# A one-core decoder-layer kernel: the first element's key transposes and scores move into the last steps of the prompt attention, and GpSimd's queue is reordered

## What is computed

```python
# prompt: causal, over its own 512 keys
s = einsum('bqhmd,bkhmd->bhmqk', qi, k) * scale
w = softmax(s)[:, :, 0] - lam * softmax(s)[:, :, 1]
o = einsum('bhqk,bkhv->bqhv', w, v)
# sample: 8 elements, each with 1024 past keys in 8 pages and 8 new ones
k_past = cache_k[l, page_table]; v_past = cache_v[l, page_table]
w = _diff_weights(concatenate([s_past, s_new]), lam)
o = w[..., :P] @ v_past + w[..., P:] @ v_new
# both: a root mean square norm over each head's 128 values
o = o * rsqrt(mean(o * o) + LN_EPS) * g * (1 - lam_init)
```

## Time and profile before

| | us |
|---|---|
| Median of 3 runs | 699.65 |
| The profiled execution, its own time | 696.74 |
| Its span, first to last instruction | 695.1 |
| Matmuls on TensorE, busy | 604.1 (87%) |
| VectorE, busy | 267.1 (38%) |
| ScalarE, busy | 158.5 (23%) |
| GpSimd, busy | 104.5 (15%) |
| TensorE's share of the chain that ended last | 67% |

### The profile page before, as it was taken

The page is one execution under the profiler, slowest core; times in us unless marked ns, Lnnn a source line. Parts: engine busy times, 40 slices in busy tenths (PEclk is TensorE's granted clock), DMA queues, the critical chain, the costliest instruction groups (busy, mean ns, idle before and its releaser), DMA issues.

```text
span 695.1 us, 10925 instructions
## 1 busy us (share of the span) xinstructions
PE 604.1 (87%) x3948; PEld 390.5 (56%) x3948; DVE 267.1 (38%) x566; ACT 158.5 (23%) x321; POOL 104.5 (15%) x189
## 2 busy tenths in 40 slices
PE   6999999997997789899999889898998777777674
PEld 5777677455666577665554546566565443444331
DVE  1562259318555555544735661111011000000267
ACT  2001452125235344341000111111111111111122
POOL 6000000012104343500100012121121111110100
PEclk9999999999999999999999899999999999999997
DMA  9630301328107889950498959999999999999683
GB/s 252 212 104 20 121 1 36 116 91 318 62 1 246 321 295 384 394 196 1 171 425 346 397 223 370 420 415 417 414 416 417 417 419 414 417 417 411 236 300 124
DMA packets 57135, 186.93 MB, mean 269 GB/s; under 512 B 10643, under 2 KB 14739, under 8 KB 48386
## 3 DMA queue, kind: packets, MB, share of 16 engines
q1 hardware_dynamic: 43440, 151.44, 56.4%
q0 software_dynamic: 11328, 29.01, 11.3%
q10 hardware_dynamic: 2322, 5.90, 2.1%
HBM read 176.80 MB, written 18.42 MB: 281 GB/s over the span
## 4 chain that ended last, share of the span: by engine, by line
PE 67%; SPq 12%; DMA 6%; DVE 6%; issue 5%; ACT 3%; ACTq 0%; POOLq 0%; DVEq 0%
PE ps L755 12%; PE ps L1081 10%; PE ps L1005 6%; PE ps L1104 6%; SPq L410 4%; PE ps L804 4%; PE ps L769 4%; PE ps L876 4%; DMA arena<-in_w_down_e_dram 4%; SPq L406 3%; PE ps L888 2%; SPq L407 2%; PE ps L912 2%; PE ps L958 2%; PE ps L1031 2%
## 5 line engine op out<-in xcount | busy, mean ns | idle before, releaser
L1081 PE MATMUL ps<-arena 128*64 128x256 f32 x1088 | 122.5, 380 | 17.8 <-DMA arena<-in_w_up_e_dram 17.0
L1081 PEld LDWEIGHTS ps<-arena 128*64 128x64 f32 x1088 | 87.8, 137 | 57.3 <-DMA arena<-in_w_up_e_dram 18.5
L1802 DVE TENSOR_TENSOR arena<-ps,arena 128x128 f32<-128x128 f32 x34 | 9.9, 291 | 203.9 <-ACT arena L1347 203.9
L755 PE MATMUL ps<-arena 128*128 128x288 f32 x352 | 85.9, 407 | 0.1
L1104 PE MATMUL ps<-arena 128*64 128x512 f32 x272 | 62.1, 597 | 23.2 <-DMA arena<-in_w_down_e_dram 10.9
L755 PEld LDWEIGHTS ps<-arena 128*128 128x128 f32 x352 | 66.7, 190 | 18.8 <-issue 0.5
L1104 PEld LDWEIGHTS ps<-arena 128*64 128x64 f32 x272 | 21.5, 136 | 52.9 <-issue 52.9
L547 POOL DMA_DIRECT2D arena<-in_cache_v_dram x64 | 34.6, 541 | 60.4 <-issue 37.8
L655 POOL DMA_INDIRECT y_rows<-arena x17 | 17.2, 1012 | 171.4 <-ACT arena L1354 154.9
L1005 PE MATMUL ps<-arena 128*128 128x512 f32 x96 | 42.7, 596 | 0.0
L876 PE MATMUL ps<-arena 128*128 128x128 f32 x256 | 36.2, 280 | 2.9 <-ACT arena L1284 2.1
(11 more groups left out here) (322 smaller groups left out, 772.8 us busy)
## 6 DMA issues: line engine op xcount, KB each, us to landing
arena<-in_w_gate_e_dram SPq DMA_DIRECT2D x34, 1024.0 KB, 16.3
arena<-in_w_up_e_dram SPq DMA_DIRECT2D x34, 1024.0 KB, 23.6
arena<-in_w_down_e_dram SPq DMA_DIRECT2D x34, 1024.0 KB, 24.7
arena<-in_cache_k_dram SPq DMA_DIRECT2D x64, 256.0 KB, 7.7
arena<-in_cache_v_dram POOLq DMA_DIRECT2D x64, 256.0 KB, 6.6
arena<-in_w_in_dram SPq DMA_DIRECT2D x4, 2048.0 KB, 8.4
arena<-in_w_out_dram SPq DMA_DIRECT2D x2, 2048.0 KB, 15.9
x_rows<-arena ACTq DMA_DIRECT2D x8, 512.0 KB, 8.8
```

Source lines behind the costliest of these rows:

```text
L755: last = mm(ps[:, b + h, 0:HALF], win[n % 2][:, k, m * P:(m + 1) * P], xT[:, k, h * HALF:(h + 1) * HALF], start=k == 0, stop=k == KD - 1)
L1081: last = mm(ps[fh * 64:fh * 64 + 64, u, 0:256], xTm[:, k, u * CAP:(u + 1) * CAP], gu[:, :, k, fh * P:(fh + 1) * P], start=k == 0, stop=k = ...
```

## The change

- Element 0's 8 pages of keys are transposed inside the rounds 7, 8 and 9 of the prompt attention (`first_keys`, three, three and two pages), into PSUM bank 5, and pages 4 and 6 into bank 3. ScalarE copies all eight (`first_keys_out`) into a new buffer `kT0`, which lies where the projections' input was.
- The 64 new keys in `kT0` and the zeros behind them are written by GpSimd. Those of `kT` are written by VectorE as before, now in `sample(0)` behind the maximum.
- Element 0's scores are issued ahead of the values of step 10. The transposes of the end states move from round 7 to round 10.
- In GpSimd's stream the first query copy comes forward, and `query(1)` and the last root (`row_scale(NT - 2)`) come ahead of `values(1)`, of the four stores and of `values(2)`. Before, `values(1)` stood in the middle of the prompt attention.

```diff
+        kT0 = area(A_XT, NH, 1152)
@@ GpSimd
             row_scale(0)
             row_scale(1)
-            values(1, lambda: q.wait_ge(s_pj, 33))
+            q.wait_ge(s_pj, 33)
+            g.tensor_copy(kT0[:, :, PAST:PAST + TS], kTn[:, :, SEQ:T]).then_inc(s_k0n, 1)
+            g.memset(kT0[:, :, PAST + TS:], 0.0).then_inc(s_k0n, 1)
             row_scale(2)
+            q.wait_ge(s_cst, 3)
+            g.tensor_copy(qcur, qd[:, 0, :, :]).then_inc(s_qc, 1)
...
+            query(1)
+            row_scale(NT - 2)
+            values(1, lambda: q.wait_ge(s_sc, 1))
             q.wait_ge(s_endc, 1)
             q.dma_start(O["h_prompt"][0], ends_out[0:1, :]).then_inc(s_out, 16)
...
             values(2, tails_free)
-            query(1)
-            row_scale(NT - 2)
             query(2)
@@ TensorE
+            def first_keys(g):
+                if g == 0:
+                    pe.wait_ge(s_kin[0], 16 * NPG)
+                    pe.wait_ge(s_pev[1], 32)
+                elif g <= 3:
+                    pe.wait_ge(s_ktc[(g - 1) % 2], (g - 1) // 2 + 1)
+                else:
+                    pe.wait_ge(s_ktc[g % 2], g // 2)
+                if g == 4:
+                    pe.wait_ge(s_exp, len(STEPS) - 1)
+                for h in range(NH):
+                    last = tr(ps[:, 3 if g >= 4 and g % 2 == 0 else 5, h * P:(h + 1) * P], kpages[0][g][:, h * P:(h + 1) * P], ident)
+                last.then_inc(s_ktp[g % 2], 1)
...
             for n in range(len(STEPS)):
...
-                if n == 7:
+                if n == 10:
                     ends_rows()
+                if n in (7, 8):
+                    first_keys(3 * (n - 7))
+                if n == 9:
+                    first_keys(6)
                 if n + 1 < len(STEPS):
                     transposes(n + 1)
+                if n in (7, 8):
+                    first_keys(3 * (n - 7) + 1)
+                if n == 9:
+                    first_keys(7)
                 values(n)
+                if n == 9:
+                    first_scores()
+                if n in (7, 8):
+                    first_keys(3 * (n - 7) + 2)
...
-            for g in range(NPG):
-                keys_transpose(0, 0, g, True)
-            pe.wait_ge(s_dc, 2)
-            sample_scores(0)
             sample(0, 0, first=True)
@@ ScalarE
+            def first_keys_out(g):
+                act.wait_ge(s_ktp[g % 2], g // 2 + 1)
+                a.copy(kT0[:, :, g * P:(g + 1) * P], ps[:, 3 if g >= 4 and g % 2 == 0 else 5, :].rearrange("p (h c) -> p h c", h=NH)).then_inc(s_ktc[g % 2], 1)
...
-            for g in range(0, NPG, 2):
-                keys_out(0, g)
@@ VectorE
-            dve.wait_ge(s_pvp, len(STEPS))
-            link(v.tensor_copy(kT[:, :, PAST:PAST + TS], kTn[:, :, SEQ:T]))
-            link(v.memset(kT[:, :, PAST + TS:], 0.0))
-            dve.sem_inc(s_dc, 1)
+            def new_keys():
...
                 v.tensor_reduce(coef[:, u:u + 1], ps[:, 0:3, 0:384], AX.XY, ALU.max, negate=True).then_inc(s_mxs, 1)
+                if first:
+                    new_keys()
...
-            for g in range(1, NPG, 2):
-                keys_out(0, g)
```

More of the change, by code:

```diff
@@ L602, in tails_free @@
                 q.wait_ge(s_dc, 2)
+                q.wait_ge(s_k0n, 2)
                 q.wait_ge(s_out, 16 * 6)
-            values(2, tails_free)
             query(1)
             row_scale(NT - 2)
+            values(1, lambda: q.wait_ge(s_sc, 1))
+            q.wait_ge(s_endc, 1)
+            q.dma_start(O["h_prompt"][0], ends_out[0:1, :]).then_inc(s_out, 16)
+            q.dma_start(O["h_sample"][0], ends_out[1:9, :]).then_inc(s_out, 16)
+            q.dma_start(O["conv_prompt"][0, 0], ends_out[9:12, :]).then_inc(s_out, 16)
+            q.dma_start(O["conv_sample"][0].rearrange("b j c -> (b j) c"), ends_out[12:36, :]).then_inc(s_out, 16)
+            values(2, tails_free)
             query(2)
@@ L851, in _, with first_scores @@
             transposes(0)
+            def first_keys(g):
[11 more added lines that the diff above has]
+                last.then_inc(s_ktp[g % 2], 1)
+            def first_scores():
+                pe.wait_ge(s_qc, 1)
+                pe.wait_ge(s_ktc[0], 4)
+                pe.wait_ge(s_ktc[1], 4)
+                pe.wait_ge(s_k0n, 2)
+                pe.wait_ge(s_exp, len(STEPS))
+                for c in range(3):
+                    for h in range(NH):
+                        last = mm(ps[32 * h:32 * h + 32, c, 0:384], qcur[:, h, :], kT0[:, h, c * 384:(c + 1) * 384], start=True, stop=True)
+                last.then_inc(s_sc, 1)
             for n in range(len(STEPS)):
@@ L856, in _, with keys_transpose @@
                     gate_half(n + 1)
-                if n == 7:
+                if n == 10:
                     ends_rows()
+                if n in (7, 8):
+                    first_keys(3 * (n - 7))
+                if n == 9:
+                    first_keys(6)
                 if n + 1 < len(STEPS):
                     transposes(n + 1)
+                if n in (7, 8):
+                    first_keys(3 * (n - 7) + 1)
+                if n == 9:
+                    first_keys(7)
                 values(n)
+                if n == 9:
+                    first_scores()
+                if n in (7, 8):
+                    first_keys(3 * (n - 7) + 2)
                 if tile_ended(n, 3) is not None:
                     o_transpose(pe, tile_ended(n, 3))
-            pe.wait_ge(s_exp, len(STEPS))
             pe.wait_ge(s_wc, len(STEPS))
-            def keys_transpose(b, u, g, first=False):
+            def keys_transpose(b, u, g):
                 if g == 0:
                     pe.wait_ge(s_kin[b % 3], 16 * NPG * (b // 3 + 1))
-                if not (first and g < 2):
-                    pe.wait_ge(s_ktc[g % 2], 4 * b + g // 2)
+                pe.wait_ge(s_ktc[g % 2], 4 * b + g // 2)
                 for h in range(NH):
@@ L1250, in _ @@
             exps(2)
+            def first_keys_out(g):
+                act.wait_ge(s_ktp[g % 2], g // 2 + 1)
+                a.copy(kT0[:, :, g * P:(g + 1) * P], ps[:, 3 if g >= 4 and g % 2 == 0 else 5, :].rearrange("p (h c) -> p h c", h=NH)).then_inc(s_ktc[g % 2], 1)
             for n in range(len(STEPS)):
+                if n in (7, 8):
+                    first_keys_out(3 * (n - 7))
+                if n == 10:
+                    ends_rows_out()
+                if n == 9:
+                    first_keys_out(6)
                 if n + 1 < len(STEPS):
                     weights_out(n + 1)
+                if n == 9:
+                    first_keys_out(7)
+                if n in (7, 8):
+                    first_keys_out(3 * (n - 7) + 1)
                 if tile_ended(n, 0) is not None:
@@ L1551, in _ @@
                     norm(tile_ended(n, 2))
-            dve.wait_ge(s_pvp, len(STEPS))
-            link(v.tensor_copy(kT[:, :, PAST:PAST + TS], kTn[:, :, SEQ:T]))
-            link(v.memset(kT[:, :, PAST + TS:], 0.0))
-            dve.sem_inc(s_dc, 1)
+            def new_keys():
+                dve.wait_ge(s_pvp, len(STEPS))
+                link(v.tensor_copy(kT[:, :, PAST:PAST + TS], kTn[:, :, SEQ:T]))
+                link(v.memset(kT[:, :, PAST + TS:], 0.0))
+                dve.sem_inc(s_dc, 1)
             step = [0]
```

15 lines of the change are left out of this document (5 added, 10 removed).

## The result

The change made the kernel slower: 706.91 us (median of 4 runs, 705.77 to 710.85) against 699.89 us for the kernel before, run beside it (4 runs, 698.48 to 700.98). The ratio, estimated over all the runs, is 1.0114, 95% interval 1.0089 to 1.0139 (the two medians alone give 1.0100). The forecast was 704.1 with a range of 701.5 to 708.0: the sign and the range hold, the likeliest case was too small. It had +4.4 us; the chip shows +7.0.

The account below looks back on a forecast made before the run. TensorE held most of the chain of waits, with GpSimd nearly full in the sample stage. GpSimd's delay of 2.98 us plus 1.45 us of clock made 4.4 on 699.65: 704.1 us, range 701.5 to 708.0.

Parts of the forecast that it names:

- the sign: Whole kernel: the change makes it slower, chance 0.85.
- the likeliest case: Whole kernel: the forecast itself, 4.4 us slower at 704.1 us, own range 703 to 706, chance 52%.
- Part 1: Prompt attention rounds 7 to 9: element 0's key transposes fit there, readers of its exponential start 3.65 us earlier.
- Part 2: Norm's last root on GpSimd: starts at 231.0 us, where it started at 234.70.
- Part 3: GpSimd between root and second query copy: reads, loads, stores and landing wait make element 2's scores 2.98 us later.
- R: Start of the norm's last root on GpSimd, forecast at 231.0 us; GpSimd's later steps are counted from it.
- The stores land late: Rival, GpSimd's queue: stores behind eight value pages land at R + 18.8, 2.7 us more, 706.8 us; chance 13%.
- Does it happen again? No: Later elements: query copies come 10.0 us apart, TensorE asks after 10.5 or more, so no further gap, by half a us.
- Part 4: TensorE behind its idle gap ahead of element 2's scores: clock falls to 1.2 GHz, 1.45 us lost.
- The clock stays up: Rival, gap ahead of element 2's scores: no clock loss, only Part 3 counts, 702.6 us; chance 15%.
- The sum: Whole kernel: 2.98 us of GpSimd's chain plus 1.45 of clock, 4.4 us slower, 704.1 us.

## Why the prediction was right and wrong

- **Part 1, the keys inside the rounds: right.** Element 0's scores were forecast at 12.4 us behind the mark (223.8) and came at 12.09; the gain at the readers of its exponential was 4.0 us for 3.65. All nine kernels show it.
- **Part 2, the root: right.** 19.65 forecast (231.0), 19.40 measured.
- **Part 3, GpSimd's chain: the mechanism right, one term mis-sized.** Pages at R + 5.0 (measured 4.99) and the last store at R + 11.3 (11.23) hold. The step that failed is "the last one starts at R + 11.3 and took 4.8, R + 16.1, and about 0.6 us to the first load: R + 16.7". The store took 7.3 us and landed at R + 18.5, so the first page went at R + 19.29, 2.6 us later than forecast; the pause of 0.40 us behind that first page, which the sum did not have, came on top. Less 0.25 us for the earlier root and 0.1 at the query, that is 2.6 us at element 2's scores.
- **The base of that term.** The 4.8 us were read from the store's own issue, 4.7 us behind the end of the page issues ahead of it (220.40 against 215.67 in the kernel before). Counted from that end, the store landed 9.5 us later, and the same count in the changed kernel gives 8.9. Taken so, the row would have given a landing at R + 19.2. So the stores of 218.80, of which the prediction says that they "do not tell", did tell.
- **The rival "The stores land late": it is what happened.** It stood at 706.8 with 13%; 706.91 was measured. Part of how close that comes is luck: the landing was 0.3 us earlier than in the rival, and the pause was in neither sum.
- **The order in the queue.** In all seven kernels with the stores behind pages (the kernel before, the changed one and five of the experiments), the last store landed 8.0 to 9.7 us after the end of the page issues and 0.7 to 1.4 us after the last page had landed, though its own issue stood 1.6 to 4.7 us behind the pages. The DMA engines' busy share over that time was 0.85 in the kernel before and 1.03 in the changed one. The Trainium skill's page "DMA: Bandwidth & Descriptors", section "Two DMAs through the same engine are not ordered", says that descriptors of one queue start in order on each engine; the landings just given agree with it. A run with the stores on another queue, which would show whether the order or the traffic holds them, was not made.
- **"Does it happen again? No": right.** The next queries come 9.24 to 9.54 us apart, where 10.0 was forecast, and TensorE's later scores wait 0.74 us.
- **Part 4, the clock: right.** 1.45 us forecast, 1.56 measured (3.70 less 2.14), and about 1.4 given back when TensorE was kept busy. It fell in the gaps of 5.31, 7.35 and 10.29 us ahead of element 2's scores, and right behind the 3.73 us ahead of element 1's in the run with the root behind the pages. This also answers the rival "The clock stays up", at 702.6.
- **The sum.** 2.98 forecast, 2.62 from the stores and the pause (element 2's scores start 44.12 us behind the mark, where 41.50 was forecast), 1.56 of clock: 7.16, where the distance to element 3's scores grew by 7.14 and the time by 7.0.
- **Not foreseen.** I had seen the page work that the change leaves between the root and the next query, but not that the reads could stand in the root's wait: the place of the root alone, with all else kept, decides over the 7 us, and so does that of the query. And of the 4 us gained at the front at most 2.4 were kept in these runs, since value pages become the next wait.

## What to carry to other kernels

When a change moves work past a queue, count everything that the queue must do before the next thing that the critical engine waits for, its register reads and its waits for landings too. A queue that looks 44% busy (4.58 of 10.50 us here) can be nearly full. Put short work, such as stores and register reads, into the time in which the engine waits for a late input. Put first in the queue what the critical engine reads, and issue what must land soon ahead of the large transfers and not behind them; price its landing from the transfers ahead of it. And look for the next limit before counting a gain: here four microseconds at the front become two, because TensorE then waits for value pages.

## What the runs showed of the hardware

- The same four small stores (2 to 48 KB) landed in 2.6 to 4.2 us with no pages right ahead of them on the queue, and in 6.2 to 8.1 us right behind eight pages of 256 KB. Counted from the end of the pages' issues, the last of them landed 8.0 to 9.7 us later, also in the kernel before, where it was issued 4.7 us behind the pages and took 4.8 us.
- GpSimd's eight register reads take 4.0 to 5.0 us between instructions and do not show as busy time. With four of the eight moved ahead of the root, 1.79 us were left between the root and the first page issue.
- One float32 matmul of 384 columns in the program is two in the trace: 14 calls left 28 and 28 left 56, 0.33 us each.
- The granted clock can be 0.51 or 1.00 in the same stretch of the same code in two executions (162.9 to 169.7). It makes some 3 us of difference between two profiles that no edit has made, and is the reason to count from a common mark.
- A gap of 3.73 us on TensorE (235.96 to 239.69 in the run with the root behind the pages) was followed by a granted clock of 0.59 from 240.0 to 243.4, and by scores of 3.79 us instead of 2.14: this short gap cost, too.
